# Adding the attention mask on VectorE, inside the search for a row's maximum, in place of mask products on TensorE

## The reference

```
logits = where(causal or in_window, logits, -inf)
p = softmax(logits)        # exp(logits - max) / sum
```

## Time and profile before

| | us |
|---|---|
| median of 3 runs (lowest, highest) | 1768.23 (1767.32, 1769.28) |
| the profiled execution | 1767.02 |
| its span | 1765.2 |
| mean granted TensorE clock | 0.968 of full |
| busy: TensorE matmul, weight load | 1678.9, 1318.3 |
| busy: VectorE, ScalarE, GpSimd | 934.0, 726.6, 383.9 |

### The profile page before, as it was taken

How to read it: one execution, slowest core, us unless ns; L and a number is a source line. 1 busy time by engine, 2 the same in 40 slices (tenths; PEclk the granted TensorE clock), 3 DMA queues, 4 the chain that set the end, 5 groups by cost and what they waited for, 6 DMA issues and landing times.

```text
span 1765.2 us, 24732 instructions
## 1 busy us (share of the span) xinstructions
PE 1678.9 (95%) x9314; PEld 1318.3 (75%) x9314; DVE 934.0 (53%) x1675; ACT 726.6 (41%) x1643; POOL 383.9 (22%) x517
## 2 busy tenths in 40 slices
PE   7999998998879998999999999999999998998979
PEld 6887766887755555888888888888887767886757
DVE  3795664356246676345343234334745774457772
ACT  4334663153336666223332123233335553534550
POOL 5441332022115654011000000000112330023330
PEclk9999998999958999999999999999999998999989
DMA  7223002423012221423322232224231003230111
GB/s 187 81 87 96 25 25 84 143 74 128 14 34 58 67 59 36 153 96 96 95 96 95 96 96 96 95 96 134 83 109 35 26 25 139 77 96 25 49 49 48
DMA packets 107206, 141.38 MB, mean 80 GB/s; under 512 B 30349, under 2 KB 55205, under 8 KB 106849
## 3 DMA queue, kind: packets, MB, share of 16 engines
q1 hardware_dynamic: 106032, 139.10, 24.8%
q0 software_dynamic: 992, 0.86, 0.5%
q10 hardware_dynamic: 80, 0.02, 0.0%
HBM read 125.24 MB, written 4.24 MB: 73 GB/s over the span
## 4 chain that ended last, share of the span: by engine, by line
PE 66%; DVE 11%; issue 10%; ACT 9%; POOL 3%; DMA 0%; ACTq 0%; SPq 0%; POOLq 0%; DVEq 0%
PE ps L2023 51%; PE ps L2477 2%; PE ps L2258 2%; DVE spl L1171 2%; DVE nm L1500 2%; ACT pbd L954 2%; PE ps L2279 2%; PE ps L2294 1%; PE ps L2432 1%; ACT pb L898 1%; ACT qkt L975 1%; PE ps L2456 1%; ACT pts L962 1%; ACT pbs L954 1%; DVE qkt L1518 1%
## 5 line engine op out<-in xcount | busy, mean ns | idle before, releaser
L2023 PE MATMUL ps<-spl,ht 128*128 128x512 f32 x2496 | 579.5, 394 | 9.2 <-DVE xk L1709 5.9
L2023 PEld LDWEIGHTS ps<-spl,ht 128*128 128x128 f32 x2496 | 473.4, 190 | 109.3 <-DVE xk L1709 6.3
L1194 DVE TENSOR_TENSOR spl<-raw,spl 128x1024 fp32r<-128x1024 f32 x168 | 222.2, 1364 | 396.8 <-ACT spl L726 396.8
L726 ACT ACTIVATE spl<-raw 128x1024 fp32r<-128x1024 f32 x168 | 168.5, 1052 | 464.1 <-PE ps L2023 437.7
L2023 PE MATMUL ps<-ht,spl 128*128 128x512 f32 x960 | 220.4, 391 | 2.0 <-DVE spl L1194 2.0
L2023 PEld LDWEIGHTS ps<-ht,spl 128*128 128x128 f32 x960 | 181.1, 189 | 40.6 <-issue 2.9
L2023 PE MATMUL ps<-spl,uu 128*128 128x512 f32 x768 | 174.7, 389 | 0.0
L2023 PEld LDWEIGHTS ps<-spl,uu 128*128 128x128 f32 x768 | 144.1, 188 | 29.9
L2477 PE MATMUL ps<-ht,spl 128*128 128x512 f32 x576 | 155.2, 408 | 2.7 <-DVE mx L1555 2.6
L2477 PEld LDWEIGHTS ps<-ht,spl 128*128 128x128 f32 x576 | 102.7, 190 | 23.8 <-DVE mx L1555 4.8
L1885 POOL TENSOR_TENSOR sq_first<-qkv 128x2048 f32<-128x2048 f32 (+1 forms) x14 | 47.9, 3423 | 316.0 <-ACT qkv L769 301.4
(11 more groups left out here) (315 smaller groups left out, 2228.2 us busy)
## 6 DMA issues: line engine op xcount, KB each, us to landing
raw<-w_in SPq DMA_DIRECT2D x30, 1024.0 KB, 5.1
raw<-w_mlp_up SPq DMA_DIRECT2D x16, 1024.0 KB, 5.2
raw<-w_mlp_down SPq DMA_DIRECT2D x16, 1024.0 KB, 5.1
raw<-w_in_a SPq DMA_DIRECT2D x16, 1024.0 KB, 5.3
raw<-w_in_b SPq DMA_DIRECT2D x8, 1024.0 KB, 5.3
raw<-w_proj_diff SPq DMA_DIRECT2D x4, 1024.0 KB, 6.2
stq<-qkv SPq DMA_DIRECT2D x16, 256.0 KB, 2.7
stq<-qkv SPq DMA_DIRECT2D x32, 128.0 KB, 2.5
```

The lines of the kernel that those rows point to most:

```text
L726: act.activation(SPL[:, n % 2, HI, 2 * k:2 * k + 2], RAW[:, n % 2, 2 * k:2 * k + 2], ACT.Copy).then_inc(hi_done, 4)
L1194: dve.tensor_tensor(SPL[:, n % 2, LO, 2 * k:2 * k + 2], RAW[:, n % 2, 2 * k:2 * k + 2], SPL[:, n % 2, HI, 2 * k:2 * k + 2].bitcast(F32), A ...
L2023: last = pe.matmul(PS[:, b0 + b], left[:, x], right[:, y], start=(kt == 0 and i == 0), stop=(kt == UK * g["units"] - 1 and i == 2))
```

## The change

In DIFF, FOX and SWA the mask products go. TensorE's last score product (in FOX the forget term) now signals the scores. VectorE's maximum becomes a fused operation on the same bank: it adds the mask to the scores, multiplies by -1, writes that back over the scores in PSUM, and keeps the minimum of it, which is the negated maximum of the masked row. ScalarE's exponential then reads negated scores and gets scale -1. The masks are slices of two tiles: `CAUSAL`, now 512 columns wide with the triangle in the last 128, and `BAND`, 258 columns: band, triangle, and zeros for the sink. NSA keeps its mask product and reads the last 128 columns of `CAUSAL`. VectorE waits for the constants ahead of the first maximum of each of the three attentions.

```diff
@@ constants
-        CAUSAL = sb("causal", [P], BF16)
-        ID64, CAUSAL64, BAND64 = [sb(x, [2, P], BF16) for x in ("id64", "causal64", "band64")]
+        CAUSAL, BAND = sb("causal", [S], BF16), sb("band", [2 * P + 2], BF16)
+        def mask_of(a, t):
+            w = a.width(t)
+            return BAND[:, 2 * P - w:2 * P + a.sink] if a.banded else CAUSAL[:, S - w:S]
@@ ScalarE, exps in attend_beside
-                                              bias=NM[:, m % 2, h, t:t + 1], accum_out=LS[:, m % 2, h, t:t + 1])
+                                              bias=NM[:, m % 2, h, t:t + 1], scale=-1.0, accum_out=LS[:, m % 2, h, t:t + 1])
@@ VectorE, maxima in attend_beside (LARGE = 3e38)
-                        dve.tensor_reduce(NM[:, m % 2, h, t:t + 1], bank[:, 0:w + a.sink], AX.X, ALU.max, negate=True)\
-                           .then_inc(s["mx"], 1)
+                        dve.tensor_tensor_reduce(bank[:, 0:w + a.sink], bank[:, 0:w + a.sink], mask_of(a, t), -1.0, LARGE,
+                                                 ALU.add, ALU.min, NM[:, m % 2, h, t:t + 1]).then_inc(s["mx"], 1)
...
+                dve.wait_ge(consts, 14)
                 maxima(0)
@@ GpSimd, the start
-            pool.memset(ID64[:], 0.0)
-            pool.memset(BAND64[:], 0.0).then_inc(consts, 1)
-            pool.memset(CAUSAL64[:], 0.0).then_inc(consts, 1)
+            pool.memset(BAND[:, 0:P], 0.0).then_inc(consts, 1)
+            pool.memset(BAND[:, P:2 * P + 2], 0.0).then_inc(consts, 1)
...
-            for h in range(2):
-                r = slice(HD * h, HD * h + HD)
-                pool.wait_ge(consts, 12 + h)
-                pool.affine_select(out=ID64[r], ...)
-                pool.affine_select(out=CAUSAL64[r], ...)
-                last = pool.affine_select(out=BAND64[r], ...)
-                last.then_inc(consts, 1)
+            pool.wait_ge(consts, 12)
+            pool.affine_select(out=BAND[:, 0:P], ...).then_inc(consts, 1)
+            pool.affine_select(out=BAND[:, P:2 * P], ...).then_inc(consts, 1)
@@ TensorE, scores_of in attend_beside
-                            pe.matmul(PS[:, score_bank(a, n, h), 0:w], QKT[r, m % 2, 0, x, P * t:P * t + P],
-                                      QKT[r, a.keys_of(m) % 2, 1, y, P * a.first_key(t):P * t + P],
-                                      start=(j == 0), stop=False, skip_group_check=True)
+                            last = pe.matmul(PS[:, score_bank(a, n, h), 0:w], QKT[r, m % 2, 0, x, P * t:P * t + P],
+                                             QKT[r, a.keys_of(m) % 2, 1, y, P * a.first_key(t):P * t + P],
+                                             start=(j == 0), stop=(j == 2 and not a.is_fox), skip_group_check=True)
+                            if j == 2 and not a.is_fox:
+                                last.then_inc(s["s"], 1)
...
-                                      start=False, stop=False, skip_group_check=True)
-                    if a.banded and t:
-                        add_mask(n, BAND64, 0, False)
-                    add_mask(n, CAUSAL64, w - P, True)
-
-                def add_mask(n, mask, col, last):
-                    for j in range(2):
-                        for h in range(2):
-                            r = slice(HD * h, HD * h + HD)
-                            done = pe.matmul(PS[:, score_bank(a, n, h), col:col + P], ID64[r, j], mask[r, j], start=False,
-                                             stop=last and j == 1, skip_group_check=True)
-                            if last and j:
-                                done.then_inc(s["s"], 1)
+                                      start=False, stop=True, skip_group_check=True).then_inc(s["s"], 1)
```

More of the change, by code:

```diff
@@ L34 @@
 MASKED = -1e30
+LARGE = 3e38
 LAMBDA_INIT = 0.2
@@ L1821, in _ @@
                                    pattern=[[-1, P]], channel_multiplier=1).then_inc(consts, 1)
-            pool.affine_select(out=CAUSAL[:], in_=CAUSAL[:], compare_op=ALU.is_ge, fill=MASKED, base=0,
+            pool.affine_select(out=CAUSAL[:, S - P:S], in_=CAUSAL[:, S - P:S], compare_op=ALU.is_ge, fill=MASKED, base=0,
                                pattern=[[-1, P]], channel_multiplier=1).then_inc(consts, 1)
@@ L1829, in _ @@
             pool.memset(ONEB[:], 1.0).then_inc(consts, 1)
[L1830 to L1839 removed]
+            pool.wait_ge(consts, 12)
+            pool.affine_select(out=BAND[:, 0:P], in_=BAND[:, 0:P], compare_op=ALU.is_ge, fill=MASKED, base=-1,
+                               pattern=[[1, P]], channel_multiplier=-1).then_inc(consts, 1)
+            pool.affine_select(out=BAND[:, P:2 * P], in_=BAND[:, P:2 * P], compare_op=ALU.is_ge, fill=MASKED, base=0,
+                               pattern=[[-1, P]], channel_multiplier=1).then_inc(consts, 1)
             pool.wait_ge(consts, 14)
@@ L2262, in scores_of @@
                         bank = PS[:, 2 * (idx % 2) + h]
-                        pe.matmul(bank[:, w - P:w], IDB[:], CAUSAL[:], start=False, stop=True,
+                        pe.matmul(bank[:, w - P:w], IDB[:], CAUSAL[:, S - P:S], start=False, stop=True,
                                   skip_group_check=True).then_inc(s["s"], 1)
```

6 lines of the change are left out of this document (removed).

## The result

| | before | after |
|---|---|---|
| median (lowest, highest), 8 runs each | 1766.6 (1765.46, 1769.28) | 1774.39 (1772.25, 1775.31) |
| the profiled execution | 1767.02 | 1774.97 |
| its span | 1765.2 | 1773.2 |
| mean granted TensorE clock | 0.968 | 0.961 |
| busy: TensorE matmul, weight load | 1678.9, 1318.3 | 1673.6, 1311.1 |

The ratio of after to before is 1.0041, with a 95% interval of 1.0031 to 1.005. So the change costs 7 to 8 us. I had forecast 1766.5 us, 1.7 us faster than the 1768.23 us known then, with a range up to 1773.5 us. The result lies outside it, on the slow side.

A forecast was written before the change was run, and what follows sets the result against it. The prediction took a VectorE-ScalarE loop as the bound, with TensorE pacing parts of fox. TensorE's -2.90 us and VectorE's +1.2 gave -1.7 us, against the median of 1768.23: 1766.5 us, range 1762.5 to 1773.5.

The forecast's parts named there:

- What bounds the kernel: Three attentions: a loop of maxima, exponential, copy, split through VectorE and ScalarE; TensorE sets the pace about once in four fox steps.
- The read-out: VectorE, after each fused operation: reading out the accumulator, 83 ns, is covered by the main operation's tail and costs nothing.
- My own sign: First maximum's start to its exponential's start: grows under 30 ns if the forecast is right, 80 ns or more if wrong.
- rival A: Maxima on the loop: the accumulator's read-out is serial, 83 ns x 78 = 6.5 us, total 1771.8 us; chance 0.17.
- The count of 78: Maxima of the touched line on the chain of waits: 28 in differential attention, 13 in fox, 37 in swa.
- the upper end of 150 ns: VectorE's highest cost per maximum: 67 ns for a pointer-scalar add plus 83 for the read-out in full, 11.7 us.
- The fused operation's own length: VectorE at 512 elements: the fused operation lasts 685 to 710 ns, against 683 for the maximum.
- TensorE's part: Three attentions: 480 mask products removed, valued by their pieces of the chain, 2.90 us gained.
- the next claimant in fox: Fox: the exponential's waits for TensorE, 1.6 us each, far over 0.3 us, so the gain there is not eaten.
- Rival D: Swa: TensorE's clock falls for 8 us, costing at most 4 us, total 1770.5 us; chance 0.06.
- My sign for D: TensorE's clock: a low clock appearing before 1688 us would show the forecast wrong and a clock fall in swa.
- Edits with one answer: Exponential's scale, VectorE's wait on constants, GpSimd's start, second attention's mask slice: each costed at nothing.

The follow-up runs named there:

- the filled pair: Kernel before and kernel after, each with six identity products in each step without a gate tile, up to the last two steps: 1758.79 and 1765.9 us.
- the fill: Six identity products added in each step without a gate tile, up to the last two, on the kernel before: 1758.79 us, ratio 0.9954.

## Why the prediction was wrong, point by point

**What bounds the kernel.** Right: the loop through VectorE and ScalarE sets the differential stage and swa, and TensorE stands in only in fox. Removing all mask products changed the unit period by nothing that counts in the first two and by 0.11 us in fox.

**The read-out: the step that failed.** "So I take the read-out as covered by the tail of the main operation." The row was read rightly, and the same holds at 512 elements with the scores in PSUM as a source: 82 ns, hidden. But the row's operation wrote to SBUF and the change's writes to PSUM. There the read-out takes 140 ns and the maximum is ready 0.06 to 0.07 us after the main operation's end. I priced the destination by itself, from a one-element write, at 4 ns. By itself it is near that (9 ns for operand and write together). The price sits in the pair, and no row of before had the pair. My parts each came from the row nearest in kind, and their sum missed what only arises when two of them meet. My own sign was the time from a first maximum's start to its exponential's start: under 30 ns more if right, 80 or more for rival A. It grew by 70 ns, in the gap between the two, and much nearer to A.

In my terms: 89 read-out pieces on the chain, 82 ns in the mean, 7.33 us, where the sum had none. The count of 78 was good, and the upper end of 150 ns for each held the truth. Rival A was the mechanism (83 ns x 78 = 6.5 us), with its place, its price and nearly its size; I gave it 0.17. Its total, 3.6 us slower, was still only half of what was measured, since it had the 2.90 us of TensorE taken off. Its reason, that a read-out has a duration of its own, was not quite the one: a read-out of the same kind is free behind a write to SBUF.

The Trainium skill, Vector Engine (DVE) Microarchitecture Reference, section 5.2, with about 75 ns per instruction after overlap, had led to an estimate of 7.0 us for VectorE's loss. The trace after has 7.33. The page's figure doesn't depend on the destination, though, and behind the write to SBUF there was no such term: the two operations of that pair start 0.61 us apart, as the plain maxima do.

**The fused operation's own length.** "Lasts 685 to 710 ns": 713, and 690 where a plain maximum precedes it. Of the 15 ns a maximum, the part for the second operand and the write held (11 forecast; 692 against 683). The rest of the 30 ns comes behind another fused operation's read-out: the first of a pair shows 0.69 us in the timeline, the second 0.73.

**TensorE's part.** The sum had 2.90 us: 0.30 in the ramp, 2.12 in fox, 0.48 in swa. Measured: 0.9 to 1.2 in fox, nothing in the other two. This is the second term that was wrong. A piece of the chain was here an upper bound of what its removal gave. I had argued that the next claimant in fox leaves room of 1.6 us, but those are five waits in 64 us, not every step. In each unit of fox's loop the chain has two mask pieces, one of 0.11 us ahead of more work of TensorE and one of 0.16 us ahead of a maximum, 0.27 us together; the unit got shorter by 0.11 to 0.12. So only part of them was worth anything, and which of the two no run tells.

**The clock.** Rival D put one fall in the middle of swa, at 4 us and a chance of 0.06. It was the right mechanism in other places: at the stages' ends, at swa's start, in the differential ramp, and from there into the projections behind. It eats what fox gave. With the products gone and nothing else changed, the ratio is 0.9998. My sign for D, a low clock before 1688 us, could not tell anything: the kernel before has one from 1600.0 to 1606.8 us already.

**Edits with one answer.** Scale -1, the wait on the constants, the wider masks, GpSimd's start and the second attention's mask: costed at nothing. Differential attention starts at 151.17 us after and at 151.43 before, by its first transposes. None of the others was tried alone, so it is only their sum in the first 151 us that is shown to be small.

**Sum.** Forecast -2.90 + 1.2. Measured in parts: VectorE +6.4 to +7.8, fox -0.9 to -1.2, the clock's part on top. The clock's part of the change can be read off the two profiled executions, which differ by 8.0 us of span. The differential ramp lost 1.24 us where a unit of its loop loses 0.27, so 1.0 is the clock's. Its end, from the last unit to the projection, lost 0.92 us (0.27 in the filled pair), so 0.65 more. The projections counted above, behind the three stages, changed by -0.36, -0.16 and +1.44 us, together 0.9. That makes some 2.6 us, and it leaves 5.4 for VectorE less fox, where the chain's 7.33 less 1.2 gives 6.1. The remaining 0.7 us has no place in this account. The 0.2 us for each us at half clock that the fill gave would make 4.8 us of the 24 more; that rate is a mean of very unlike places and doesn't carry over.

## What to carry to other kernels

When an operation is built from neighbours, look for a row with both the new property and the new destination. If none exists, keep the serial price as a live case, above all where the result of the pair is what another engine waits for. And before taking work off an engine that idles at the ends of stages, read the granted clock there and in what follows: in this kernel the cheapest 8 us were not in the loop, but in adding useless products, up to the point where TensorE's own queue sets the step, and most of them came back in the projections behind.

## What the runs showed of the hardware that was not expected

- An accumulator's read-out on VectorE takes 82 ns and is hidden behind the main operation when that writes SBUF; when it writes PSUM (here always the bank that it reads), it takes 140 ns and ends 0.06 to 0.07 us later. An operation of two operands in place in PSUM without accumulator takes 692 ns at 512 elements, against 683 for a maximum that writes one element.
- The exponential on ScalarE takes 715 ns at 512 elements with its source in SBUF, against 683 from PSUM.
- Identity products in the steps without gate tiles took the time at half clock from 47.7 to 6.9 us and 8 us off the kernel; four more of them in each step took all of that back.
- A us at half clock cost 0.47 us in the projections behind the attentions (5.2 of 11.1), and 0.10 us within the attentions (3.0 of 29.9).
